# The 64-token triangular inverses of the second block's linear attention: 16x16 diagonal blocks from one GpSimd chain through memory, two doubling levels left on TensorE

## The reference

```
A   = strictly triangular part of  (a * decay) (b / decay)^T     # 64 x 64 per chunk
T   = (I + A)^-1                                               # unit triangular
W   = T (decayed keys),   U = T (A_k v)                        # A_k: the same product with k
then a scan over the 8 chunks that carries a 64 x 64 state a head
```

## Time and profile before

| | us |
|---|---|
| median of 3 runs | 2848.72 (2847.73 to 2853.95) |
| the profiled execution | 2848.62, of which 2847.3 are the span from first to last instruction and 1.3 lie around it |
| TensorE busy, whole span | 2709.7 (95%) |
| solve stage, from the first `low` product to the last fed step | 1839.9 to 1964.9, 125.0 us |
| GpSimd busy in the solve stage | 33.0 |

### The profile page before, as it was taken

The page is one execution under the profiler, slowest core; times in us unless marked ns, Lnnn a source line. Parts: engine busy times, 40 slices in busy tenths (PEclk is TensorE's granted clock), DMA queues, the critical chain, the costliest instruction groups (busy, mean ns, idle before and its releaser), DMA issues. The chain is left out here.

```text
span 2847.3 us, 34735 instructions
## 1 busy us (share of the span) xinstructions
PE 2709.7 (95%) x13981; PEld 2222.3 (78%) x13981; DVE 1653.8 (58%) x2699; ACT 1217.9 (43%) x1981; POOL 200.3 (7%) x240
## 2 busy tenths in 40 slices
PE   6999999999999898899999999999999999999998
PEld 5777788887887787688877776797797767788887
DVE  6786563545864774444588887433415487544444
ACT  3666422223446354334577774422224356332222
POOL 0000000000003630200000011031100001000001
PEclk9999999999999999899999999999999999999999
DMA  6233264432232220635699992211321215222322
GB/s 241 87 135 112 97 224 154 151 141 93 89 126 77 72 86 1 238 126 185 232 353 360 353 374 78 80 45 67 116 103 37 75 56 187 87 100 86 104 85 71
DMA packets 82201, 390.44 MB, mean 137 GB/s; under 512 B 17067, under 2 KB 21071, under 8 KB 46287
## 3 DMA queue, kind: packets, MB, share of 16 engines
q1 hardware_dynamic: 68624, 352.09, 34.4%
q10 hardware_dynamic: 10382, 26.07, 2.6%
q0 software_dynamic: 3024, 9.98, 1.0%
HBM read 368.96 MB, written 24.39 MB: 138 GB/s over the span
## 5 line engine op out<-in xcount | busy, mean ns | idle before, releaser
L342 DVE TENSOR_TENSOR wlo<-stage,whi 128x1024 fp32r<-128x1024 f32 (+3 forms) x481 | 515.3, 1110 | 317.1 <-ACT whi L354 314.9
L354 ACT ACTIVATE whi<-stage 128x1024 fp32r<-128x1024 f32 (+3 forms) x481 | 437.5, 956 | 215.1 <-PE ps L694 184.3
L694 PE MATMUL ps<-whi,mxhi 128*128 128x512 f32 (+1 forms) x528 | 204.5, 387 | 9.9 <-DVE wlo L342 7.8
L694 PE MATMUL ps<-bxhi,whi 128*128 128x512 f32 x480 | 199.5, 416 | 8.7 <-DVE y0lo L342 4.0
L694 PE MATMUL ps<-whi,mxlo 128*128 128x512 f32 (+1 forms) x528 | 197.9, 375 | 0.0
L694 PE MATMUL ps<-wlo,mxhi 128*128 128x512 f32 (+1 forms) x528 | 197.9, 375 | 0.0
L694 PE MATMUL ps<-bxhi,wlo 128*128 128x512 f32 x480 | 189.1, 394 | 0.0
L694 PE MATMUL ps<-bxlo,whi 128*128 128x512 f32 x480 | 188.4, 393 | 0.0
L342 DVE TENSOR_TENSOR wlo<-more,whi 128x1024 fp32r<-128x1024 f32 (+1 forms) x126 | 142.8, 1175 | 58.7 <-ACT whi L354 58.1
L354 ACT ACTIVATE whi<-more 128x1024 fp32r<-128x1024 f32 (+1 forms) x126 | 121.6, 1015 | 50.1 <-PE ps L694 44.8
L694 PE MATMUL ps<-lxhi,whi 128*128 128x512 f32 x352 | 140.5, 399 | 1.6 <-DVE lxlo L350 1.6
(11 more groups left out here) (630 smaller groups left out, 6084.3 us busy)
## 6 DMA issues: line engine op xcount, KB each, us to landing
stage<-in_gu SPq DMA_DIRECT2D x92, 1024.0 KB, 6.3
more<-in_gu SPq DMA_DIRECT2D x40, 1024.0 KB, 6.9
stage<-in_ada SPq DMA_DIRECT2D x39, 1024.0 KB, 4.9
stage<-in_dn SPq DMA_DIRECT2D x19, 1024.0 KB, 7.0
stage<-in_dn SPq DMA_DIRECT2D x24, 768.0 KB, 4.4
stage<-in_gin SPq DMA_DIRECT2D x16, 1024.0 KB, 5.0
stage<-in_gt SPq DMA_DIRECT2D x16, 1024.0 KB, 5.0
more<-in_dn SPq DMA_DIRECT2D x13, 1024.0 KB, 7.0
```

Source lines behind the costliest of these rows:

```text
L342: return e.do.tensor_tensor(out, x, y, op)
L354: return e.do.activation(out, x, f, **kw)
L694: return self.p.do.matmul(out, lhsT, rhs, start=start, stop=stop, skip_group_check=True)
```

## The change

In the solve stage of the second block the levels 2, 4 and 8 are taken from TensorE. SP stores the four `R.A[h]` to memory (256 KB each), reads their 16x16 diagonal blocks into `U16` (half of the tile `sq`) by 16 transfers of 8 KB, GpSimd inverts all of them in one chain of 30 small operations, SP stores the result (4 x 32 KB) and reads it back by rows (4 transfers); for each head one 128x512 operation makes `TT` from it, and levels 16 and 32 go on as before. A head now has stages 0 to 5, the heads start in rounds 0, 1, 2 and 6, and there are 12 rounds. Three or four steps follow each round instead of two. The `low` products are reordered: kind 0 of all heads first, then kinds 2, 1, 3 of each head; three steps are fed a head instead of two, and eight instead of four before the rounds. The number of steps in the stage stays at 64. The constant `blk16` replaces `lev1`, `lev2`, `lev4`, `lev8` (384 columns fewer of constants), and the first block uses it in place of the mask that it built. `branches_sync` is called later in the program text; SP's own order changes only by the two new parts, `blocks()` ahead of everything of `GATES[1]` and `inverses()` between its first and second piece.

```diff
@@ constants
-    for s in (1, 2, 4, 8, 16, 32, 64):
+    c["blk16"] = ((i // 16) == (j // 16)) * 1.0
+    for s in (16, 32, 64):
@@ gdn_inverse (first block)
-                tt(g, L.blk, self.c("lev1"), self.c("lev2"), ADD).then_inc(*G.up())
-                for k in (4, 8):
-                    g.wait_ge(G.now())
-                    tt(g, L.blk, L.blk, self.c(f"lev{k}"), ADD).then_inc(*G.up())
-                g.wait_ge(G.now())
-                tt(g, L.blk, self.c("ident"), L.blk, SUB).then_inc(*G.up())
@@ branches_sync
+        def blocks():
+            R = L.R
+            for h in range(4):
+                s.wait_ge(self.A(free(("low", 0, h))))
+                s.do.dma_start(tri[h, 0:65536].rearrange("(p n) -> p n", p=P), R.A[h]).then_inc(*D[h].up("written", by=16))
+            for h in range(4):
+                s.wait_ge(D[h]("written"))
+                diag = tri[h, 0:8 * 8208].rearrange("(b x) -> b x", b=8)[:, 0:8192].rearrange("b (j y) -> b j y", j=16)
+                for c in range(4):
+                    q = 32 * h + 8 * c
+                    s.do.dma_start(R.U3[q:q + 8], diag[:, :, c * P:c * P + 16]).then_inc(*D[h].up("blocks", by=16))
+
+        def inverses():
+            R = L.R
+            s.wait_ge(self.G("rtri"))
+            for h in range(4):
+                s.do.dma_start(triq[h].rearrange("(p n) -> p n", p=32), R.Q16[32 * h:32 * h + 32, :]).then_inc(*D[h].up("inverses", by=16))
+            for h in range(4):
+                s.wait_ge(D[h]("inverses"))
+                s.do.dma_start(R.comp[h], triq[h].rearrange("(c p i) -> p c i", c=4, i=16)).then_inc(*D[h].up("rows", by=16))
+
         for g, ids in enumerate(GATES):
+            if g == 1:
+                blocks()
             for p in ids:
+                if g == 1 and p == ids[1]:
+                    inverses()
                 self.sync_load(self.place["gt", p] + NST + 1)
@@ rwkv
-        begin = (0, 2, 4, 12)
-        R.rounds = [[(h, r - begin[h]) for h in range(4) if 0 <= r - begin[h] < 12] for r in range(24)]
+        begin = (0, 1, 2, 6)
+        R.rounds = [[(h, r - begin[h]) for h in range(4) if 0 <= r - begin[h] < 6] for r in range(12)]
+        R.fed = [24]
+        for r in range(12):
+            R.fed.append(R.fed[r] + (4 if r % 3 == 1 else 3))
@@ rwkv_solve_pe
-            for s in S:
-                for n in range(4):
-                    z = self.mm(b[n][:, s], R.BK[hp, m, n // 2, s], R.AR[hp, m, n % 2, s])
-            z.then_inc(*P_.up(*(("low", n, h) for n in range(4))))
-            feed(2)
+            for s in S:
+                z = self.mm(b[:, s], R.BK[hp, m, 0, s], R.AR[hp, m, 0, s])
+            z.then_inc(*P_.up(("low", 0, h)))
+        for h in range(4):
+            m, hp, hc = R.head(h)
+            for n in (2, 1, 3):
...
+            feed(3)
...
-        feed(4)
-        for live in R.rounds:
+        feed(8)
+        for r, live in enumerate(R.rounds):
...
-            feed(2)
+            feed(R.fed[r + 1] - R.fed[r])
@@ rwkv_solve_act
+        gates = Flow(self.flow_act(L, GATES[1], L.zr[0], 2))
+        for h in range(4):
+            m, hp, hc = R.head(h)
             a.wait_ge(P_(("uk", h)))
             act(a, R.U[:, :, hc], ...)
-        gates = Flow(self.flow_act(L, GATES[1], L.zr[0], 2))
+            gates.run(4 + 3 * h)
         for r, live in enumerate(R.rounds):
-            gates.run(14 + 2 * r)
+            gates.run(R.fed[r], 4 if r == 0 else 2)
@@ rwkv_solve_pool
+        g.do.memset(R.Q16, 0.0).then_inc(*G.up())
+        g.wait_ge(G.now())
+        g.do.memset(R.Q16[:, 0:256:17], 1.0).then_inc(*G.up())
+        g.wait_ge(*(self.Drt[h]("blocks") for h in range(4)))
+        for k in range(15):
+            size = [P, k + 1, 15 - k]
+            prod = R.prod[:, 0:size[1] * size[2]].rearrange("p (r i) -> p r i", r=size[1])
+            g.wait_ge(G.now())
+            tt(g, prod, R.Q3[:, 0:k + 1, k].unsqueeze(2).broadcast_to(size), R.U3[:, k, k + 1:16].unsqueeze(1).broadcast_to(size), MUL).then_inc(*G.up())
+            g.wait_ge(G.now())
+            tt(g, R.Q3[:, 0:k + 1, k + 1:16], R.Q3[:, 0:k + 1, k + 1:16], prod, SUB).then_inc(*G.up(*(["rtri"] if k == 14 else [])))
         for live in R.rounds:
             for h, st in live:
                 if st == 0:
-                    tt(g, v4(TT), v4(R.A[h]), lev(1), MUL).then_inc(*G.up())
-                    g.wait_ge(G.now())
-                    tt(g, v4(TT), v4(TT), ident, ADD).then_inc(*G.up(("rtt", h)))
+                    g.wait_ge(P_(("uk", 3)), self.Drt[h]("rows"))
...
+                    tt(g, TT.rearrange("p (c b i) -> p c b i", c=4, b=8), comp, mask, MUL).then_inc(*G.up(("rtt", h)))
```

More of the change, by code:

```diff
@@ L1634 @@
 class Gdn:
[L1637 removed]
+    LEVELS = (16, 32, 64)
     def gdn(self):
@@ L3027, in branches @@
         self.Dg, self.Dr = [self.sem(f"gate{i}") for i in range(4)], [self.sem(f"regate{i}") for i in range(4)]
+        self.Drt = [self.sem(f"rtri{h}") for h in range(4)]
         L.zr = [self.at(n, [P, 4, 512], o) for n, o in (("zr0", 99.15), ("zr1", 87.15))]
-        self.branches_sync(L)
         self.middle_pe(L)
@@ L3901, in rwkv_solve_pe @@
             m, hp, hc = R.head(h)
-            b, vac = zip(*(self.take(("low", n, h)) for n in range(4)))
-            for marks in vac:
-                p.wait_ge(*marks)
+            b, vacant = self.take(("low", 0, h))
+            p.wait_ge(*vacant)
             for s in S:
-                for n in range(4):
-                    z = self.mm(b[n][:, s], R.BK[hp, m, n // 2, s], R.AR[hp, m, n % 2, s])
-            z.then_inc(*P_.up(*(("low", n, h) for n in range(4))))
-            feed(2)
+                z = self.mm(b[:, s], R.BK[hp, m, 0, s], R.AR[hp, m, 0, s])
[3 more added lines that the diff above has]
+            for n in (2, 1, 3):
+                b, vacant = self.take(("low", n, h))
+                p.wait_ge(*vacant)
+                for s in S:
+                    z = self.mm(b[:, s], R.BK[hp, m, n // 2, s], R.AR[hp, m, n % 2, s])
+                z.then_inc(*P_.up(("low", n, h)))
+            feed(3)
             ps, vacant = self.take(("uk", h))
@@ L3925, in rwkv_solve_pe @@
                     z.then_inc(*P_.up(("rt", h)))
-                elif st == 11:
+                elif st == 5:
                     (b1, v1), (b2, v2) = self.take(("rw1", h)), self.take(("ru", h))
-                    p.wait_ge(V(("rTT", h, 10)), *v1, *v2)
+                    p.wait_ge(V(("rTT", h, 4)), *v1, *v2)
                     for i, s in enumerate(S):
@@ L4015, in rwkv_solve_pool @@
                 if st == 0:
-                    g.wait_ge(P_(("uk", 3)), A(free(("low", 0, h))))
-                    if h >= 3:
-                        g.wait_ge(P_(("ru", h - 3)))
-                    tt(g, v4(TT), v4(R.A[h]), lev(1), MUL).then_inc(*G.up())
-                    g.wait_ge(G.now())
-                    tt(g, v4(TT), v4(TT), ident, ADD).then_inc(*G.up(("rtt", h)))
-                elif st % 2 and st < 11:
-                    if st > 1:
-                        g.wait_ge(P_(("rTT", h, st - 1)))
-                    tt(g, v4(B), v4(R.A[h]), lev(self.LEVELS[st // 2]), MUL).then_inc(*G.up(("rlev", h, st)))
+                    g.wait_ge(P_(("uk", 3)), self.Drt[h]("rows"))
+                    if h == 2:
+                        g.wait_ge(self.Drt[3]("inverses"))
+                    if h == 3:
+                        g.wait_ge(P_(("ru", 0)))
+                    comp = R.comp[h].unsqueeze(2).broadcast_to([P, 4, 8, 16])
+                    tt(g, TT.rearrange("p (c b i) -> p c b i", c=4, b=8), comp, mask, MUL).then_inc(*G.up(("rtt", h)))
+                elif st in (1, 3):
+                    g.wait_ge(A(free(("low", 0, h))))
+                    if st == 3:
+                        g.wait_ge(P_(("rTT", h, 2)))
+                    tt(g, v4(B), v4(R.A[h]), lev(16 if st == 1 else 32), MUL).then_inc(*G.up(("rlev", h, st)))
     def rwkv_scan_pe(self, L, R):
```

41 lines of the change are left out of this document (22 added, 19 removed).

## The result

| | us |
|---|---|
| changed kernel, median | 2819.56 (2817.52 to 2822.24, 4 runs) |
| kernel before, run beside it | 2850.32 (2847.73 to 2853.95, 4 runs) |
| ratio | 0.9891, interval [0.9875, 0.9906] |
| predicted | 2817.5 (2813.5 to 2825.0) |
| profiled execution of the changed kernel | 2822.24, span 2820.9 (the slowest of its four) |

The account below looks back on a forecast made before the run. TensorE, busy without a hole for the solve stage's 125.0 us, was taken as the bound. From 2848.62 us, 32.0 for instructions + 0.6 for fewer changes - 1.5 of wait gave 31.1 less: 2817.5 us, range 2813.5 to 2825.

Parts of the forecast that it names:

- 288 instructions at 0.111 us, 32.0: Solve stage, TensorE: three levels' matmuls for four heads go, 288 instructions at 0.111 us, 32.0 us less.
- Fewer changes between kinds of work, 0.6 in a range of 0 to 1.9: Solve stage, TensorE: twelve rounds fewer save twelve changes to and from steps, nothing to 1.9 us, taken as 0.6.
- TensorE asks for the first `TT` 32.7 us after the stage's start (1872.6 - 1839.9): Solve stage: after low products, `uk` and steps, TensorE wants to transpose the first `TT` at 1872.6.
- The chain at 1852 to 1864: Solve stage, GpSimd: 30 small operations take 11.82 us once blocks land at 1851.8, done at 1863.6, nine us ahead of TensorE.
- if GpSimd starts the chain after 1857: Solve stage: a sign that the prediction is wrong, the chain of 30 being expected at 1852 to 1864.
- The queue: SP: inverses stand behind piece 5's second-bank store, go out at 1868.6, reach TensorE 5.26 us later; wait taken as 1.5.
- No idle time in the rounds, clock 1.00, what is queued behind: Solve stage: answers arrive within rounds, granted clock 1.00 throughout, loads queued on SP have over 20 us cover; nothing lost.
- First block: nothing: First block: five GpSimd 128x128 operations go ahead of a 1.58 us idle wait for blocks; worth nothing.
- The sum: Whole kernel: 32.0 + 0.6 - 1.5 = 31.1 us less than 2848.62, so 2817.5 us.
- A long wait: Rival at the first spread: late chain idles TensorE 4 to 10 us, clock costs 2 to 3; 2822 to 2829; chance 0.13.
- Not faster: Rival: the wait at the first spread eats the whole gain, needing 2.7 us per block read; chance 0.06.
- it doesn't do what it says: Rival, solve stage: if TensorE were not the bound, 288 instructions fewer would bring nothing; held excluded by stretches without a hole.

Follow-up runs that it names:

- the idle instructions: Changed kernel with 288 fp32 matmul instructions put back on TensorE in stage 2, repeating `rT`, repetitions unread: 2853.95 us in a single execution.
- the order alone: Kernel before with only the changed kernel's order of low products and steps, all five levels left on TensorE: 2852.97 us, ratio 1.0009.
- the two kernels made to test it: Changed kernel with the first block's mask built again on GpSimd: 2821.2 us; changed kernel with early inverses, paired low products, twelve steps ahead, four idle GpSimd additions: 2815.71.
- late inverses: Changed kernel with SP sending the inverses one gate store later, behind the first bank of piece 6: 2832.33 us in a single execution.
- the double chain: Changed kernel with GpSimd's chain of 30 operations run twice before SP may go: 2835.55 us in a single execution.
- serial reads: Changed kernel with SP waiting for each of the sixteen block reads before issuing the next: 2834.65 us in a single execution.
- the pairs: Changed kernel with low products of kinds 2, 1, 3 made for two heads alternating, six steps behind each pair: 2814.64 us, ratio 0.9866.
- the joined one: Changed kernel with inverses one gate store earlier, low products by pairs of heads, twelve steps instead of eight ahead of the rounds: 2814.38 us, again 2813.04.

## Why the prediction was right, point by point

*288 instructions at 0.111 us, 32.0.* Right: the idle instructions cost 32.2. This is the mechanism of the forecast, and it carries nearly the whole gain.

*Fewer changes between kinds of work, 0.6 in a range of 0 to 1.9.* TensorE's work in the stage fell by 125.0 - (91.65 - 0.9) = 34.2 us. Without the 32.0 and the 0.7 that the order alone saved, 1.5 is left for them (1.3 with the 32.2 measured): nearer the upper bound. The sum also had no term for the order: the low products take 13.7 us where they took 4 x 3.76 = 15.0.

*TensorE asks for the first `TT` 32.7 us after the stage's start (1872.6 - 1839.9).* It was 1876.1 - 1844.58 = 31.5. The step that was off is "kind 0 of four heads is a quarter of 4 x 3.76": its 32 instructions took 5.06 - 2.88 = 2.2 us, not 3.76, because the earlier trace rows show a head alone, in one half of the array. The Trainium skill (TensorEngine Tiling (Array Packing), "Key Properties") says that different tiles can do their weight loads and matmuls in parallel; by that rule, the trace agrees, with 0.07 us an instruction across the halves where one half alone has 0.12, and I had not weighed it.

*The chain at 1852 to 1864.* It started 12.5 us after the stage's start (1857.12) and not 11.9: the reads could begin 1.1 us sooner, since kind 0 was, but the sixteen took 7.07 us to issue, 0.44 each, where I had 0.34 from the earlier trace rows. It took 10.5 us and not 11.8; beside it VectorE had five masks of 0.69 us and no split. Done 23.1 us after the start against 23.7 forecast. Taken by the letter, my sign of being wrong "if GpSimd starts the chain after 1857" came true; the whole stage began 4.7 us later than before, and counted from the stage's start the bound would be 17.1 us, the chain's start 12.5.

*The queue.* Right in its mechanism: SP held the inverses for 4.4 us behind the gate store. From their issue to TensorE 5.13 us (1872.03 to 1877.16), forecast 5.26; the hops behind a gate store were not slower. The wait was 0.9 where I took 1.5 with bounds of 0 and 4, and with the inverses earlier it was none.

*No idle time in the rounds, clock 1.00, what is queued behind.* Right, in every row of the stage.

*First block: nothing.* This failed in the traces. The chain there had the same start as before relative to GpSimd's work ahead of it, but in the changed kernel an instruction load falls on a store, and TensorE's wait grew from 3.62 to 5.16 us. From one weight load ahead of the first block's attention to one behind it (issued at 783.9 and 1187.8 us before), the eleven profiles with a late store take on average 2.6 us longer than before (0.6 to 7.3), the two others 1.0 and 1.9, which lies inside that spread. The medians of the two kernels made to test it did not fall, so that its share in the time is only argued.

*The sum.* Stage 2.2 us shorter than forecast (91.7 for 93.9), yet the time 2.1 us longer (2819.56 for 2817.5). The sum stood on one execution of before, 2848.62, and that was a fast one: in the four sets of runs the medians of before were 2850.32, 2853.39, 2851.89 and 2852.41. Those less 33.3 give 2817.0 to 2820.1, and 1 or 2 us of the first block would lie on top. Two errors of 2 us cancelled, so that the number came out nearer than the sum deserved: that part is luck. In the profiled pair the rest of the span is 6.9 us longer than before: 1.6 up to the first of the two weight loads named above, 3.2 from there to the second, and 2.3 behind the stage, less 0.1 in between. Behind the stage there is no new wait of TensorE (25.7 us in all, before 25.9), as the prediction had it, but some 300 us on the granted clock is 0.74 over 20 us where the same 20 us of before have 0.91, behind the same wait of 1.95 us:

```profile
2231.00:2251.00 20.00, 18.20 (x79) 13.05 (x80) 14.91 (x40) 8.11 (x25) 0.00 (x0) 0.74 0.04 14
```

Why the clock stays low for longer there, no run shows. Of the 1.6 at the start the clock shows the nature too, granted 0.89 before and 0.86 after in the first 60 us, and 0.94 in the second profile of the same changed kernel:

```profile
0.00:60.00 60.00, 38.79 (x144) 29.66 (x145) 38.16 (x71) 18.49 (x25) 2.01 (x5) 0.86 0.70 278
```

```profile
0.00:60.00 60.00, 38.90 (x164) 29.54 (x165) 40.22 (x75) 20.80 (x29) 2.01 (x5) 0.94 0.69 278
```

*The rivals.* "A long wait" did not come, but its price was right: 6.1 us of wait with 2.2 for the clock in the kernel with late inverses, 9.4 with 2.3 for the double chain, where I had 4 to 10 with 2 to 3. "Not faster" was excluded by serial reads at 1.8 us each, where it needed over 2.7, and "it doesn't do what it says" by the idle instructions.

## What to carry to other kernels

Where windows show an engine without a hole, count its instructions and take the pace from start to start; then look for the first place where the new producer must have delivered, and read the in-order queue there: what stands ahead of the transfer decides when it leaves, not when the data is ready. A chain taken off the bound engine costs nothing as long as its result arrives before that engine asks. When TensorE came to ask sooner (the pairs, a hole of 3.8 us), four steps more ahead of the rounds closed the hole (1.4 us, and none in the second profile). Compare small effects by the stage in the trace and put the sum against a median of many executions, not the one that was profiled.

## What the runs showed of the hardware that was not expected

- Matmuls of 64 rows that alternate between the two halves of the partitions run at 0.06 to 0.07 us an instruction, those in one half at 0.12. All low products take 5.06 + 3 x 2.88 = 13.7 us in the changed kernel and 5.4 + 2.9 = 8.3 in the joined one; with the hole of 0.9 these are 6.3 of the 6.8 us between them.
- Waits of TensorE of 0.9 and 1.4 us left the granted clock at 1.00. Behind waits of 3.8, 6.1, 9.4 and 16.5 us it was 0.50 for another 2.7, 4.9, 5.0 and 4.6 us and then 1.00 again, and the stage was longer by 1.0, 2.2, 2.3 and 2.1 us besides the wait: past 6 us, a longer wait cost no more of it.
- Small GpSimd operations of 0.2 to 0.3 us took 1.08 to 1.29 while VectorE's split of two inputs ran. The Trainium skill (SBUF — State Buffer, "SBUF: two separate sides") has the ports that VectorE and GpSimd share as an exclusive lock, which one of them holds for a whole instruction; by that rule, the trace agrees: a split is 1.2 us long.
- An instruction load of one packet, 0.9 to 1.8 us of one DMA engine, went with a 256 KB store whose reads started 2.6 to 4.2 us behind it instead of 2.0. It is the neighbourhood in time, in fourteen profiles, that speaks for it; no run took the load away.
